# Linear attention of the second block placed between the panels of its input projection, with heads computed in token rows

## The reference, cut to what matters

```
proj = u @ w_in                                  # 272 x 2064: pool_v 512, q 256, k 256, v 512, r 512, g_lr 16
log_a = log_sigmoid(g_lr @ w_gate_up + b_gate) / 16
b = cumsum(log_a) in each chunk of 64 tokens     # 4 heads, keys of 64, values of 128 per head
q_t, k_t, k_end = q / 8 * exp(b), k * exp(-b), k * exp(b_last - b)
scores = tril(q_t @ k_t.T)                       # 64 x 64 for each chunk and head
dS = k_end.T @ v
S[n + 1] = exp(b_last) * S[n] + dS[n]            # 64 x 128 for each head
o = scores @ v + q_t @ S[n]
o = o * rsqrt(mean(o * o) + eps) * gla_norm_w * silu(r)
y_pool = ((window means of pool_v) - pool_v) @ pool_w * pool_scale
h = h + concat(y_pool, o) @ w_out
h = h + mixture_of_experts(rmsnorm(h))
```

## Time and profile before

| what | value |
|---|---|
| median of 3 runs | 2132.88 us |
| the profiled execution, its own time | 2130.97 us |
| span of the profiled execution | 2129.3 us |
| TensorE matmul busy | 2033.7 us (96%) |
| VectorE busy | 1479.8 us (69%) |
| ScalarE busy | 1016.9 us (48%) |
| mean granted TensorE clock | 0.98 |

### The profile page before, as it was taken

One profiled execution on the slowest core, in us unless ns is written; L12 is line 12 of the kernel. 1 busy time (PEld: TensorE's weight loads), 2 busy tenths in 40 slices (PEclk: granted clock), 3 DMA queues, 4 the chain that ended last, 5 costly groups with the idle time before them and its releaser, 6 DMA issues.

```text
span 2129.3 us, 31696 instructions
## 1 busy us (share of the span) xinstructions
PE 2033.7 (96%) x12110; PEld 1757.4 (83%) x12110; DVE 1479.8 (69%) x2244; ACT 1016.9 (48%) x1701; POOL 19.6 (1%) x41
## 2 busy tenths in 40 slices
PE   6999999999999999999996789999999999999998
PEld 4698888888887798888885679999999988888886
DVE  3578668587667588768586878888877774755554
ACT  5362323237666562323235766445555563544443
POOL 0100000000000000000001000000000000000000
PEclk9999999999999999999998999999999997999999
DMA  7857445432111146447653207775365542355552
GB/s 294 327 183 236 144 159 167 151 116 85 60 60 60 59 159 218 140 156 259 237 157 79 75 21 247 247 265 184 119 195 178 163 154 81 119 185 191 181 193 92
DMA packets 254662, 340.40 MB, mean 160 GB/s; under 512 B 24407, under 2 KB 233138, under 8 KB 251458
## 3 DMA queue, kind: packets, MB, share of 16 engines
q1 hardware_dynamic: 254530, 338.60, 48.0%
HBM read 337.52 MB, written 1.05 MB: 159 GB/s over the span
## 4 chain that ended last, share of the span: by engine, by line
PE 79%; DVE 9%; ACT 7%; issue 4%; DMA 0%; DVEq 0%; POOL 0%; ACTq 0%; SPq 0%
PE bank L1670 24%; PE bank L1671 23%; PE bank L1672 23%; PE bank L2453 4%; DVE w_lo L2521 1%; ACT p_raw L1294 1%; ACT w_hi L947 1%; ACT p_raw L1282 1%; DVE p_all L3027 1%; DVE norm L2547 1%; PE bank L1741 1%; PE bank L1722 1%; ACT norm L1039 1%; ACT mp_raw L1460 1%; DVE neg_max L3036 1%
## 5 line engine op out<-in xcount | busy, mean ns | idle before, releaser
L2521 DVE TENSOR_TENSOR w_lo<-w_raw,w_hi 128x1024 fp32r<-128x1024 f32 x443 | 540.4, 1222 | 124.6 <-ACT w_hi L1626 85.2
L947 ACT ACTIVATE w_hi<-w_raw 128x1024 fp32r<-128x1024 f32 x350 | 367.8, 1053 | 380.6 <-PE bank L1672 372.5
L1670 PE MATMUL bank<-h_hi,w_hi 128*128 128x512 f32 (+3 forms) x1360 | 466.4, 343 | 17.7 <-DVE h_lo L2557 10.0
L1671 PE MATMUL bank<-h_lo,w_hi 128*128 128x512 f32 (+3 forms) x1360 | 459.5, 338 | 0.0
L1672 PE MATMUL bank<-h_hi,w_lo 128*128 128x512 f32 (+3 forms) x1360 | 459.3, 338 | 0.0
L1670 PE MATMUL bank<-g_hi,w_hi 128*128 128x256 f32 (+1 forms) x1216 | 403.4, 332 | 6.8 <-DVE g_lo L3081 3.6
L1671 PE MATMUL bank<-g_lo,w_hi 128*128 128x256 f32 (+1 forms) x1216 | 399.5, 328 | 0.0
L1672 PE MATMUL bank<-g_hi,w_lo 128*128 128x256 f32 (+1 forms) x1216 | 399.3, 328 | 0.0
L1670 PEld LDWEIGHTS bank<-h_hi,w_hi 128*128 128x128 f32 x1360 | 257.1, 189 | 57.7 <-issue 17.5
L1672 PEld LDWEIGHTS bank<-h_hi,w_lo 128*128 128x128 f32 x1360 | 257.1, 189 | 27.6
L1671 PEld LDWEIGHTS bank<-h_lo,w_hi 128*128 128x128 f32 x1360 | 257.4, 189 | 26.8 <-issue 0.6
(11 more groups left out here) (473 smaller groups left out, 2914.9 us busy)
## 6 DMA issues: line engine op xcount, KB each, us to landing
w_raw<-in_mlp_w SPq DMA_DIRECT2D x128, 1024.0 KB, 5.6
mod_raw<-in_mod_w SPq DMA_DIRECT2D x96, 768.0 KB, 4.7
first_raw<-in_mod_w SPq DMA_DIRECT2D x24, 1024.0 KB, 5.4
w_raw<-in_w_expert_gate SPq DMA_DIRECT2D x32, 512.0 KB, 4.0
w_raw<-in_w_expert_up SPq DMA_DIRECT2D x32, 512.0 KB, 5.0
w_raw<-in_w_expert_down SPq DMA_DIRECT2D x16, 1024.0 KB, 4.9
w_raw<-in_diff_w_qkv SPq DMA_DIRECT2D x12, 1024.0 KB, 5.2
w_raw<-in_fourier_w SPq DMA_DIRECT2D x8, 1024.0 KB, 7.3
```

Source lines behind the costliest of these rows:

```text
L947: act.activation(split_panel(W_hi[n % RING], n), raw_panel(n), ACT.Copy).then_inc(s("w_hi"), 1)
L1670: pe.matmul(dst, w_hi, r_hi, start=start, stop=False)
L1671: pe.matmul(dst, w_hi, r_lo, start=False, stop=False)
L2521: dve.tensor_tensor(split_panel(W_lo[n % RING], n), raw_panel(n), split_panel(W_hi[n % RING], n).bitcast(F32), ALU.subtract).then_inc(s("p ...
```

## The change

The order of the panels becomes gate, values, queries, keys, pool, r. The mixer's products are placed between the panels: `turned_values` after panel 6, `turned_keys` and `scores` after 9, `states` after 10, `head_outputs` after 13, `pool_products` after 15, and only `turned_heads` after 16.

The head outputs are now one product for each chunk and head. Its stationary operand `qs` holds, along 128 partitions, the 64 gated query features and the 64 masked scores of the chunk. Its moving operand `vs` holds the 64 state rows and the 64 value rows. So 16 products of 128 moving columns (32 records) replace 32 products of 64. The result has tokens along partitions. ScalarE sums squares along the row (`accum_out`), a root and a reciprocal of 8 columns follow, and VectorE scales the rows from the bank. Then 8 transposes (`turned_heads`) bring them back to feature rows, and one VectorE instruction for each pair of heads applies `gla_norm_w` and silu(r). To place scores and values in the right half of the partitions, half of the turns of values and keys are products with the identity and not transposes.

ScalarE's exponentials become `decays`, after `split_hi` of panel 8. VectorE's `gated_qk` is divided into `gated_queries` (after `project(7)`) and `gated_keys` (after `project(8)`), and the clearing of `q_pad` goes. The states are computed by halves of the partitions: 4 copies and 12 multiply-adds where there were 2 and 6. The pool part goes from its bank straight to `Y_hi` and `Y_lo`. The final scale of the residual's columns is spread over other iterations. GpSimd masks the scores inside `qs`.

```diff
-WIN_ORDER = [16, 4, 5, 6, 7, 8, 9, 10, 11, 0, 1, 2, 3, 12, 13, 14, 15]
+WIN_ORDER = [16, 8, 9, 10, 11, 4, 5, 6, 7, 0, 1, 2, 3, 12, 13, 14, 15]
...
+for _what, _signal, _values in (("gate", "z_in", (1, 2)), ("turn_v", "v_rows", (2, 4, 5)), ("turn_k", "k_rows", (1, 2)),
+                        ("score", "sc_in", (2,)), ("state", "states", (8, 16)), ("out", "o_rows", (1, 2)),
+                        ("pool", "y_lo", (1, 2)), ("turn_o", "y_gla", (1, 2))):
...
+Y_hi = sb("Y_hi", [P, KT, TOK], F32R, over=at["x"])[:, :, LAT:TOK]
+r_silu = proj[:, R_AT:R_AT + 4, META:]
+y_f = sb("y_f", [P, 4, LAT], over=at["z_f"])
+o_rows2 = sb("o_rows2", [P, 2, GLA_HEADS, P], over=at["norm2"])
+qs = [sb(f"qs{j}", [P, 2, 4, CHUNK]) for j in range(2)]
+vs = [sb(f"vs{j}", [P, 2, 4, P]) for j in range(2)]
+k_rows = sb("k_rows", [P, 2, 3, HALF])
...
+def key_half(j):
+    return slice(j * HALF, (j + 1) * HALF)
+
+def row_half(j):
+    return slice((1 - j) * HALF, (2 - j) * HALF)
...
+    for j in range(2):
+        pool.wait_ge(s("sc_in"), j + 1)
+        masked = qs[j][row_half(j), :, :, :].rearrange("p i n c -> p (i n) c")
+        pool.affine_select(out=masked, in_=masked, compare_op=ALU.is_ge, fill=0.0, base=0,
+                           pattern=[[0, 8], [1, CHUNK]], channel_multiplier=-1).then_inc(s("sc_masked"), 1)
...
@@ scalar engine
             split_hi(p0 + i + AHEAD)
             if i == 3:
                 gates()
+            if i == 5:
+                decays()
+            if i == 7:
+                turned_values()
             if i == 10:
-                turned_values()
+                turned_keys()
             if i == 14:
-                turned_keys()
+                head_squares()
+            if i == 16:
+                pool_rows()
...
+    def decays():
         act.wait_ge(s("b_step"), 3)
...
+            for j in range(2):
+                act.activation(vs[j][row_half(j), i, :, :].rearrange("p n c -> p (n c)"), ps[row_half(j), :],
+                               ACT.Copy).then_inc(s("v_rows"), 1)
+        ps = mix_tile("turn_v", 2)
+        act.activation(v_rows_m[:, :, :].rearrange("p n c -> p (n c)"), ps[0:META, :], ACT.Copy).then_inc(s("v_rows"), 1)
...
+        ps = mix_tile("turn_k", 0)
+        act.activation(k_rows[:, :, :, :].rearrange("p i n c -> p (i n c)"), ps[:, 0:6 * HALF], ACT.Copy).then_inc(s("k_rows"), 1)
+        ps = mix_tile("turn_k", 1)
+        act.activation(k_rows_m[:, :, :].rearrange("p i c -> p (i c)"), ps[0:META, 0:2 * P], ACT.Copy).then_inc(s("k_rows"), 1)
+        ps = mix_tile("score", 0)
+        act.wait_ge(s("qk_t"), 2)
         for j in range(2):
+            act.activation(qs[j][row_half(j), :, :, :].rearrange("p i n c -> p (i n c)"), ps[row_half(j), :],
+                           ACT.Copy).then_inc(s("sc_in"), 1)
+    def head_squares():
+        for t in range(2):
+            ps = mix_tile("out", t)
+            for h in range(GLA_HEADS):
+                ins = act.activation(o_square[:, t, h, :], ps[:, h * P:(h + 1) * P], ACT.Square, accum_out=o_ss[:, t, h:h + 1])
+            ins.then_inc(s("o_norm"), 1)
+        act.wait_ge(s("o_norm"), 2)
+        act.activation(o_ss[:, :, :], o_ss[:, :, :], ACT.Sqrt, bias=eps[:, 0:1], scale=1.0 / P).then_inc(s("o_norm"), 1)
+    def pool_rows():
         for i in range(2):
             ps = mix_tile("pool", i)
             for g in range(2):
+                ins = act.activation(Y_hi[:, 2 * i + g, :], ps[:, g * LAT:(g + 1) * LAT], ACT.Identity,
                                      scale=vcol("pool_scale_2", 2 * i + g))
+            ins.then_inc(s("y_hi"), 1)
         for i in range(2):
+            act.wait_ge(s("proj"), 15 + 2 * i)
+            pair = slice(2 * i, 2 * i + 2)
+            act.activation(r_silu[:, pair, :], r_silu[:, pair, :], ACT.Silu).then_inc(s("r_silu"), 1)
+    def mixer_rest():
         for i in range(2):
             pair = slice(2 * i, 2 * i + 2)
-            act.wait_ge(s("go_step"), 2 * i + 3)
-            act.activation(y_f[:, pair, :], r_silu[:, pair, :], ACT.Identity, scale=vcol("gla_norm_w_2")).then_inc(s("go_g"), 1)
-            act.wait_ge(s("go_g"), i + 2)
+            act.wait_ge(s("y_gla"), i + 1)
             act.activation(Y_hi[:, 4 + 2 * i:6 + 2 * i, :], y_f[:, pair, :], ACT.Copy).then_inc(s("y_hi"), 1)
@@ tensor engine
+    def turned(dst, src, one, j):
+        return pe.transpose(dst, src, one) if j else pe.matmul(dst, src, one, start=True, stop=True)
+        pe.wait_ge(s("proj"), 5)
+        for i in range(2):
+            ps = mix_tile("turn_v", i)
+            for j in range(2):
+                for n in range(4):
+                    c0, cn = CHUNKS[n + 1]
+                    ins = turned(ps[row_half(j), n * P:(n + 1) * P], proj[:, V_AT + 2 * i + j, c0:c0 + cn], ident[:, :], j)
             done(ins)
+        ps = mix_tile("turn_v", 2)
         for h in range(GLA_HEADS):
             ins = pe.transpose(ps[0:META, h * P:(h + 1) * P], proj[:, V_AT + h, 0:META], ident[:, :])
         done(ins)
     def turned_keys():
         pe.wait_ge(s("k_end"), 1)
+        ps = mix_tile("turn_k", 0)
+        for i in range(2):
+            for j in range(2):
+                for n in range(3):
+                    c0, cn = CHUNKS[n + 1]
+                    at_n = (3 * i + n) * HALF
+                    ins = turned(ps[row_half(j), at_n:at_n + HALF], k_end[key_half(j), i, c0:c0 + cn],
+                                 ident[key_half(j), key_half(j)], j)
+        done(ins)
+        ps = mix_tile("turn_k", 1)
+        for i in range(2):
+            ins = pe.transpose(ps[0:META, i * P:(i + 1) * P], k_end[:, i, 0:META], ident[:, :])
+        done(ins)
+    def scores():
+        pe.wait_ge(s("qk_t"), 2)
+        ps = mix_tile("score", 0)
+        for i in range(2):
+            for j in range(2):
+                for n in range(4):
+                    c = slice(n * CHUNK, (n + 1) * CHUNK)
+                    at_n = (4 * i + n) * CHUNK
+                    ins = pe.matmul(ps[row_half(j), at_n:at_n + CHUNK], k_t[key_half(j), i, c], qs[j][key_half(j), i, n, :],
+                                    start=True, stop=True)
+        done(ins)
+    def states():
+        pe.wait_ge(s("v_rows"), 5)
+        pe.wait_ge(s("k_rows"), 2)
+        for i in range(2):
+            ps = mix_tile("state", i)
+            for n in range(4):
+                for j in range(2):
+                    keys = k_rows_m[:, i, key_half(j)] if n == 0 else k_rows[row_half(j), i, n - 1, :]
+                    values = v_rows_m[:, 2 * i + j, :] if n == 0 else vs[j][row_half(j), i, n - 1, :]
+                    ins = pe.matmul(ps[key_half(j), n * P:(n + 1) * P], keys, values, start=True, stop=True)
+            done(ins)
+    def head_outputs():
+        pe.wait_ge(s("sc_masked"), 2)
+        pe.wait_ge(s("states"), 16)
+        for t in range(2):
+            ps = mix_tile("out", t)
+            for h in range(GLA_HEADS):
+                i, j = h // 2, h % 2
+                for half in range(2):
+                    ins = pe.matmul(ps[half * CHUNK:(half + 1) * CHUNK, h * P:(h + 1) * P], qs[j][:, i, 2 * t + half, :],
+                                    vs[j][:, i, 2 * t + half, :], start=True, stop=True)
+            done(ins)
+    def pool_products():
         for i in range(2):
             ps = mix_tile("pool", i)
...
                                 start=True, stop=True)
             done(ins)
+    def turned_heads():
+        pe.wait_ge(s("o_rows"), 2)
         for i in range(2):
+            ps = mix_tile("turn_o", i)
             for j in range(2):
+                for t in range(2):
+                    ins = pe.transpose(ps[:, j * LAT + t * P:j * LAT + (t + 1) * P], o_rows2[:, t, 2 * i + j, :], ident[:, :])
             done(ins)
     p0, t0 = PLAN.at["win"]["panel"], PLAN.at["win"]["tile"]
...
             panel_product(p0 + i, t0 + i, H_hi, H_lo, slice(0, TOK2))
         if i == 2:
             gates()
+        if i == 6:
+            turned_values()
+        if i == 9:
+            turned_keys()
+            scores()
         if i == 10:
+            states()
+        if i == 13:
+            head_outputs()
+        if i == 15:
+            pool_products()
+    turned_heads()
+    first_products([p0, p0 + 1, p0 + 2], t0, Y_hi, Y_lo, slice(0, LAT), lambda k: pe.wait_ge(s("y_lo"), k // 2 + 1))
@@ vector engine
+    def final_scale():
+        dve.wait_ge(s("meta_a"), 6)
+        dve.reciprocal(final_rstd[:, :], final_rstd[:, :]).then_inc(s("meta_v"), 1)
...
+    def gated_queries():
+        dve.wait_ge(s("e_end"), 1)
+        dve.wait_ge(s("proj"), 7)
         for j in range(2):
+            half = key_half(j)
+            ins = dve.scalar_tensor_tensor(qs[j][half, :, :, :].rearrange("p i n c -> p i (n c)"), proj[half, Q_AT:Q_AT + 2, META:],
+                                           HALF ** -0.5, e_pos[half, :, META:], ALU.mult, ALU.mult)
+        ins.then_inc(s("qk_t"), 1)
+    def gated_keys():
```

(86 more changed lines are left out.)

146 lines of the change are left out of this document (18 added, 128 removed).

## The result

The changed kernel takes 2102.14 us (median of 4 runs, 2100.22 to 2103.45) against 2132.95 for the kernel before on the same chip: ratio 0.9854, 95% interval 0.9843 to 0.9866. I had forecast 2105.5 in a range of 2100 to 2113. The profiled execution took 2103.45 us (span 2101.6).

What follows compares the result with a forecast made beforehand. TensorE's chain was taken as the bound: its terms from panel 3 to VectorE's first output-product addition sum to 67.0 us against 94.3, so 2130.97 - 27.3 = 2103.7 profiled; with 1.9 added, forecast 2105.5 us, range 2100 to 2113.

Steps and rivals of the forecast that it cites:

- Chain and cover: Panel 3 to VectorE's first output-product addition: TensorE's work alone sets 67.0 us against 94.3; VectorE and ScalarE keep up.
- starts: Six groups between panels begin with a wait and change the shape: about 0.1 us in and out, 1.2 us.
- output tile: Output product's first tile, complete with matmul 66 of 72, at full clock: 8.1 us.
- Head outputs: 32 records between panels at 0.11 us, the price of the turns of values: 3.5 us, bounds 2.3 and 5.8.
- rival B: Small products on TensorE are cheaper, running at the states' 0.073 us or overlapping: 2100 to 2103 us, chance 0.12.
- Values and keys: Turns between panels: `turned_values` 28 records at 0.11, 3.1 us; `turned_keys` 1.4 us.
- Stalls: TensorE's waits for `w_lo` inside the panels, 2.26 and 1.45 us, both gone: 3.7 us.
- Margins: Near the stage's end: `turned_heads` margin 5 us, slice 4 margin 2.4, `project(16)` possibly half a microsecond late.
- Rival D: VectorE or ScalarE becomes late and panels wait as before: +3.7, up to 6 us, 2109 to 2111 us, chance 0.09.
- A: Rival: the clock falls once in the projection, costing about 12 us: 2117 us, chance 0.10.
- E: Rival: clock falls at `turned_values` and groups keep it down until the experts: 15 us slower, 2147 us, chance 0.02.
- The upper bound of 0.18: Head outputs' price per record from above, taken from the old head products: 5.8 us.

Runs made afterwards that it cites:

- halves: Changed kernel with the loops over half and head exchanged in the head outputs, four products per half together; 2102.47 us, ratio 0.9857.
- before_decays: Kernel before with only the exponentials of decays two iterations later on ScalarE and `gated_qk` one later on VectorE; 2127.55 us, ratio 0.9978.
- placed_all: Kernel before with old products and old norm placed between panels, head outputs and squares in two halves; 2129.52 us, ratio 0.9989.
- swap_twice: Changed kernel with head-output operands exchanged and each product issued twice, accumulated in the bank; 2108.36 us, ratio 0.9886.
- placed_grouped: `placed_all` with all 64-row products ahead of the 128-row ones in each bank of head outputs; 2122.14 us, ratio 0.9953.
- late: Changed kernel with keys, scores, states, head outputs and pool products moved behind panel 16; new form and norm kept; 2111.51 us, ratio 0.9898.
- before_grouped: Kernel before with all 64-row products ahead of the 128-row ones in each bank of head outputs; 2127.29 us, ratio 0.9972.
- before_placed: Kernel before with old scores, states, head outputs and pool products placed between panels, norm chain left after panel 16; 2134.74 us, ratio 1.0009.
- swap_rows: `swap_twice` with the first of each two products contracting only its first 64 rows, so 64 and 128 rows alternate; 2117.19 us, ratio 0.9927.

## Why the prediction was right

- **Chain and cover.** TensorE's line decided, as I had it. Panels 55.7 us without groups 12.5 is 43.2 (predicted 42.3 and 1.2 for starts), output tile 1794.03 - 1785.90 = 8.1 (8.1), turned heads 0.8 (1.1).
- **Groups.** 12.5 us against 14.3. Head outputs: 1.9, predicted 3.5. This is the term that was mis-sized most. I took the turns' 0.11; the 0.073 of the states was the nearer row, since both are products and not transposes, and both alternate the half of the array. The alternation explains 0.6 of the 1.6 us (`halves` takes 2.6); why a record of `halves` takes 0.080 and one of the turns 0.11 stays open. So rival B happened in part (scores 1.5 of 2.1, pool 1.5 of 1.8). Values and keys were dearer, 3.4 and about 1.9 against 3.1 and 1.4. With the starts and the turned heads, 0.3 us less each, the sum is 2.4 us: 67.0 predicted, 64.6 measured. That the profiled execution came within 0.3 us of my 2103.7 is luck: its stage was 2.4 us shorter than predicted and began 2.3 us later than in the kernel before. The median was 3.4 us below the forecast.
- **Stalls.** 3.7 us gone, and `before_decays` shows that moving the exponentials and `gated_qk` alone does it; dividing `gated_qk` and dropping the clearing weren't needed.
- **Margins.** `Y_lo` of the first pair ends at about 1788.3 (half of its row), and slice 4 begins at 1785.90 + 36 x 0.12 = 1790.2: 1.9 us against 2.4 predicted. `o_rows` was ready at 1781.56 and needed at 1785.11: 3.6 against 5. Both held; each was smaller than I had worked out. `project(16)` stood behind `pool_low` and began at 1785.66, 0.4 us behind the end of panel 16, and only ScalarE's silu of the last pair waited for it, as foreseen. Rival D did not happen.
- **The clock.** 1.00 throughout the stage: rivals A and E did not happen. My price for A was too high: 23.9 us of matmuls at 0.21 in place of 0.12 us are 10.2 us lost, not 12. My reason was incomplete, too. I argued from the length of groups and the panels around them. `placed_all` has dense panels around its groups and lost the clock 3 us into the first and right behind the second; `swap_twice` kept it for 7.3 us. As far as one trace of each shows, what protects the changed kernel is also that products of one height follow each other.
- **The upper bound of 0.18** was taken from the old head products as a price of their form. It was the price of switching. As a bound it did no harm; as an explanation it would have been wrong.

Where the 29.7 us come from: the old work placed between panels with its order mended is worth 12.9 (94.3 to 81.4). The other 16.8, from `placed_grouped` to the changed kernel, are the stalls (3.7), head outputs of 1.9 in place of 8.0 us (6.1), and the stretch behind panel 16, 1795.2 to 1811.06, or 15.9, in place of 8.9 us (7.0). The other groups between the panels cancel within 0.4 us. In `placed_grouped` the stretch holds a wait of 5.83 us for `Y_lo`:

```profile
1801.20 0.55 PE L1691 MATMUL bank<-Y_hi,w_hi 128*128 128x256 f32 x1 [5.83 <-DVE Y_lo L3416]
```

Placement by itself was worth 9.3 us in the new form (`late` to the changed kernel) and 8.4 in the old one with its order mended (`before_grouped` to `placed_grouped`), but 2.7 us at most in the old order. So what made it pay is that products of one height follow each other, which the new form brings too. What the new form is worth without placement is read from `late`: 20.4 us less than before, of which 3.7 are the stalls. The new products and the new norm were not changed one without the other.

## What to carry to other kernels

Count the switches between products of different contracted height (64 and 128 rows here) on TensorE's line, not only its records: group the products by height, or restack the operands so that one product of full height does the work of two. Put small products between dense ones only after that. In `before_placed` the products moved and the chain behind them stayed at the end, and nothing was gained; the low clock has a part in that which was not separated.

## Unexpected in the hardware

- Products of 64 and 128 contracted rows in turn: 0.11 to 0.13 us for each switch (0.36 a product in the earlier trace rows against 0.227 in `swap_twice` and 0.25 in `placed_grouped`), and the clock fell to 0.50 some 3 us (`before_placed`, `placed_all`) and 5.3 us (`swap_rows`) into such a group, and right behind another of 5.8 us (`placed_all`), with a dense panel, or a panel and four small products, ahead of it and TensorE's matmul records busy throughout. That is one trace of each kernel.
- An accumulating product on the place of the one before it costs no more than any other: 0.113 us a record against 0.115.
- Products on alternate halves of the array: 0.059 us a record of 128 columns against 0.080 when 8 records go to one half and then 8 to the other, and 0.036 against 0.048 for 64 columns. Transposes and products that take turns, on alternate halves, are dearer than one kind after the other: 4.8 against 3.2 us for 24 records, 2.6 against 1.6 for 18.
